# The V blocks of the dense PEER part, issued from ScalarE's DMA queue in place of SyncE's

## The reference, cut to what matters

```python
e = (take_along_axis(si[:, :, 0], ci // 16) * 128 + take_along_axis(si[:, :, 1], ci % 16))
gate = softmax(top)                                     # 128 experts a token
act = gelu(einsum('tkd,td->tk', peer_u[e], ub))         # d = 1024
out = einsum('tk,tkd->td', gate * act, peer_v[e])
```

## Time and profile before

| what | value |
| --- | --- |
| median of 3 runs | 6679.44 us |
| lowest and highest | 6656.4 and 6680.77 us |
| the profiled execution, its own time | 6678.65 us |
| its span, first to last instruction | 6676.6 us |
| mean granted clock of PE | 0.856 of full speed |
| PE, DVE, ACT, POOL busy | 82%, 57%, 18%, 28% |
| gathers (queue q0) | 671.13 MB |
| SP's transfers (queue q1) | 441.96 MB |
| ACT's transfers (queue q10) | 47.99 MB |

### The profile page before, as it was taken

The page is one execution under the profiler, slowest core; times in us unless marked ns, Lnnn a source line. Parts: engine busy times, 40 slices in busy tenths (PEclk is TensorE's granted clock), DMA queues, the critical chain, the costliest instruction groups (busy, mean ns, idle before and its releaser), DMA issues.

```text
span 6676.6 us, 62677 instructions
## 1 busy us (share of the span) xinstructions
PE 5486.7 (82%) x22755; PEld 3635.5 (54%) x22755; DVE 3833.7 (57%) x8953; ACT 1192.3 (18%) x2559; POOL 1875.6 (28%) x1700
## 2 busy tenths in 40 slices
PE   8899877868757779999997899887786668788876
PEld 3699454735554334554552489744655555455554
DVE  1554163737267898876674355342737376766555
ACT  1100032221373000000002110021312450000001
POOL 0000000000487564554551000000001584444442
PEclk9899978778856889999998889899567768898988
DMA  6000101012115999999995200001012249999996
GB/s 210 14 1 1 38 1 32 1 32 63 64 76 238 387 397 389 387 392 358 387 389 206 86 1 1 13 26 32 1 32 64 79 173 374 349 367 369 359 347 245
DMA packets 290066, 1165.07 MB, mean 175 GB/s; under 512 B 24416, under 2 KB 106592, under 8 KB 205024
## 3 DMA queue, kind: packets, MB, share of 16 engines
q0 software_dynamic: 92160, 671.13, 24.9%
q1 hardware_dynamic: 192272, 441.96, 18.9%
q10 hardware_dynamic: 5328, 47.99, 1.7%
HBM read 1116.94 MB, written 44.04 MB: 174 GB/s over the span
## 4 chain that ended last, share of the span: by engine, by line
PE 63%; DMA 13%; DVE 13%; ACT 5%; issue 4%; POOL 1%; ACTq 0%; DVEq 0%; SPq 0%; POOLq 0%
PE psum L413 63%; DMA weight_ring<-in_ut 12%; DVE arena L1261 3%; ACT y_features L975 2%; ACT arena L903 2%; DVE arena L1540 1%; DVE arena L1615 1%; DVE arena L1270 1%; DVE arena L1264 1%; DVE u_features L1267 1%; DVE x_tokens L1261 1%; DVE arena L1382 1%; DVE arena L1267 0%; ACT y_features L977 0%; DVE arena L1357 0%
## 5 line engine op out<-in xcount | busy, mean ns | idle before, releaser
L413 PE MATMUL psum<-u_features,weight_ring 128*128 128x256 f32 (+2 forms) x6464 | 2014.4, 471 | 345.3 <-DMA weight_ring<-in_ut 313.8
L413 PEld LDWEIGHTS psum<-u_features,weight_ring 128*128 128x128 f32 x6464 | 1312.0, 205 | 1074.3 <-DMA weight_ring<-in_ut 361.8
L413 PE MATMUL psum<-weight_ring,consts 128*128 128x512 f32 x2560 | 1141.8, 593 | 2.6 <-DMA weight_ring<-in_uv 1.9
L413 PE MATMUL psum<-arena 128*128 128x64 f32 (+5 forms) x7136 | 983.5, 320 | 45.5 <-DVE arena L1540 23.9
L413 PEld LDWEIGHTS psum<-arena 128*128 128x128 f32 (+2 forms) x7136 | 842.1, 218 | 131.2 <-issue 32.1
L1248 POOL DMA_INDIRECT arena<-in_uv,arena x560 | 833.4, 1488 | 160.4 <-POOL arena L1244 87.2
L413 PEld LDWEIGHTS psum<-weight_ring,consts 128*128 128x128 f32 x2560 | 484.8, 190 | 540.6 <-issue 491.2
L1762 DVE SCALAR_TENSOR_TENSOR y_features<-arena,y_features 128x1024 f32<-128x1024 f32 x560 | 718.0, 1282 | 12.0
L1747 DVE CUSTOM_DVE_ANT_0 arena<-arena,y_features 128x1024 f32<-128x1024 f32 x560 | 665.1, 1219 | 36.7 <-DMA arena<-in_uv,arena 36.6
L1244 POOL TENSOR_TENSOR arena<-consts 128x1 f32<-128x1 f32 x320 | 343.4, 1073 | 1148.5 <-DVE y_features L1762 1125.9
L1230 POOL TENSOR_SCALAR y_features<-consts 128x128 f32<-128x128 f32 x640 | 525.8, 838 | 463.1 <-ACT consts L965 267.7
(11 more groups left out here) (194 smaller groups left out, 5123.1 us busy)
## 6 DMA issues: line engine op xcount, KB each, us to landing
weight_ring<-in_ut SPq DMA_DIRECT2D x256, 512.0 KB, 8.8
weight_ring<-in_uv SPq DMA_DIRECT2D x256, 512.0 KB, 8.6
weight_ring<-in_ws SPq DMA_DIRECT2D x234, 512.0 KB, 3.6
gate_blocks<-arena ACTq DMA_DIRECT2D x20, 2048.0 KB, 6.3
consts<-gate_blocks SPq DMA_DIRECT2D x16, 768.0 KB, 17.3
arena<-gate_blocks SPq DMA_DIRECT2D x16, 768.0 KB, 18.3
arena<-in_uv,arena POOLq DMA_INDIRECT x560, 10.4
consts<-gate_blocks SPq DMA_DIRECT2D x16, 512.0 KB, 15.5
```

Source lines behind the costliest of these rows:

```text
L413: return pe.matmul(o, w, x, start=first, stop=last, skip_group_check=True)
```

## The change

`load_down` moves from SP's program to ACT's. V of block `e` is issued by ACT right behind the gelu of block `e`, for `e` of 2 and more; ACT has at that point already waited for "block added" of `e - 2`, so the buffer is free. V of blocks 0 and 1 is issued by ACT before its first gather group, behind a wait for the weight pieces of the layer. SP keeps a wait for "block added" of `e - 2` where the V load stood, so U loads and gate loads are issued after the same events as before. Sizes, buffers and semaphores are the same.

```diff
@@ SP's program
-                def load_down(e):
-                    if e >= 2:
-                        sp.wait_ge(*at("block added", l, e - 2))
-                    r = l * EXPERTS + e * P
-                    sp.dma_start(DOWN[e % 2], a["uv"][r:r + P, D:2 * D]).then_inc(down_in[e % 2], 16)
...
-                for e in range(2):
-                    load_down(e)
...
                 for e in range(2, BLOCKS):
                     if e + 2 < BLOCKS:
                         load_up(e + 2)
-                    load_down(e)
+                    sp.wait_ge(*at("block added", l, e - 2))
                     if e % QUAD == 2 and 2 <= e // QUAD + 1 < BLOCKS // QUAD:
                         load_gates(e // QUAD + 1)
@@ ACT's program
+            def load_down(l, e):
+                r = l * EXPERTS + e * P
+                act.dma_start(DOWN[e % 2], a["uv"][r:r + P, D:2 * D]).then_inc(down_in[e % 2], 16)
+
             def block_activated(l, e):
...
                 activated(act.activation(HID[e % 2][:, 0:hi - lo], bank(6 + e % 2, 0, hi - lo), ACT.Gelu), "block activated", l, e)
+                if e >= 2:
+                    load_down(l, e)
...
                 gate_weights(l, gather_tiles(l)[0])
+                act.wait_ge(SEM["piece_used"], (l + 1) * PIECES)
+                for e in range(2):
+                    load_down(l, e)
```

## The result

| | before | after |
| --- | --- | --- |
| median | 6680.1 us (4 runs, 6656.4 to 6687.43) | 6853.46 us (4 runs, 6803.99 to 6862.06) |
| ratio, with its 95% interval | | 1.025 (1.0194 to 1.0307) |
| span of the profiled execution | 6676.6 us | 6843.7 us |

The change makes the kernel 2.5% slower. I had forecast 36 us less, 6643 us in a range of 6601 to 6732; it is 173 us more, above the range.

A forecast was written before the change was run, and what follows sets the result against it. PE was taken to wait for U behind slow gate loads, with DMA bytes binding the first stretch. Savings of 30 us in layer 1, 4 and 2 in the second stretch made 36 us off 6678.65: 6643 us, range 6601 to 6732.

The forecast's parts named there:

- What bounds the kernel: Dense parts of both layers: PE waits for U, which stands behind gates slowed by many small packets beside gathers.
- What the change removes: At each gate load, the V 0.37 us ahead no longer delays it; 2.6 us of gather turns can go.
- V moves ahead of the late U: Behind a gate load, V(e + 1) and V(e + 2) may pass U: 2.6 us earlier to 3.0 later, about 1 earlier expected.
- My bound from above: Layer 1's DMA share could rise from 0.92 to 0.97, 60 us; with 18 of the second stretch, 78 us, 6601 us.
- V passes the late U everywhere: Rival, 0.11: two V blocks go ahead of U, 1.7 us later at each of 29 waits, 49 us, 6728 us.
- the second stretch of layer 0: 2556 to 3562 us, PE the bound: 1 us off each of 4 waits, 2 more for sooner U issues.
- ACT is held at the V issue: Rival, 0.11: V issues behind gate loads block ACT, gather gelus and V come late; about 100 us, 6779 us.
- V's cover: PE work before down(e) needs V: 15.5 us in layer 0, 9.8 in layer 1; nothing booked, range widened.
- the bytes moved: Queues: q10 carries about 134 MB more and q1 as much less.
- nothing in the first stretch: 2107 to 2556 us, first gathered tile of layer 0: no gain, as unchanged bytes set the time at DMA share 0.99.
- Nothing to gain: Rival, 0.36: U as late as before, the saving cancelled by V passing U or used up by gathers; 6679 us, within 33.
- the spacer reading: Reading tested in the experiments, not in the prediction: the V ahead of the gate load did some good there.

The follow-up runs named there:

- Long rows: Gate loads read one row of 4 or 6 KB a partition in place of 8 or 12 of 512 bytes, against the kernel before; 6506.41 us, 0.9754.
- 0.8% and 2.6% alone: Against the kernel before: only the V directly ahead of each gate load on ACT, 1.0078; only the other three of each four on ACT, 1.0262.

## Why the prediction was wrong

**What bounds the kernel: right.** U is late because it stands behind the gates, and these are slow because they are many small packets. Long rows, which change nothing but the number of packets (and the pieces of the stores before the dense part), took U waits from 313.8 to 89.7 us and 2.5% off the time. That was the gain in this place, not the queue.

**What the change removes: not there.** I put 2.6 us of gather turns on V ahead of the gates, and booked 1 us of them. With only that V moved, the gates of layer 1 landed 1.5 us earlier (15.8 for 17.3), yet U waits didn't fall (315.9 for 313.8). V and gates share the engines either way.

**The failed step: "V moves ahead of the late U", a range of 2.6 us earlier to 3.0 later, from which I chose 1 us earlier.** Three things in it were wrong. I let V(e + 1) and V(e + 2) cost U "up to 1.5 us" each, as work of their own. But they delay the gates first: while a gate load is under way, its packets share the engines with gathers and now with V as well, and in the cycle shown three V blocks went through: the one that had stood ahead of the gates and the two from behind U. The gates come 6.7 us later in layer 1, and U behind them: 6 us later in the cycle shown, where I had it 1 us earlier. Second, I judged that V(e + 1) starts when the gates are "nearly through", 7 us after them; they took 15 to 17 us, so they were half way. The row was on the table: 15.6 us in the earlier trace rows. Third, I took U waits as the whole price. The gates are needed too: DVE's waits for them went from 169.6 us to 371.8 us in all.

**Missed: what is behind a late transfer is free time that no one can use.** In the old order V stood behind U, so when the gates were through the engines had U, V and gathers to carry and stayed full (1.02 in the 8.9 us behind U's landing). Now U and V have landed, and the gathers have stopped too, since DVE was held by the late gates and POOL by DVE: the engines stand at 0.02 for 3.9 us. That late gates also hold the gathers is in none of my sums. My bound from above asked how far the DMA share could rise (0.92 to 0.97); it fell to 0.87. By 1155 us x 0.92 / 0.87 = 1221 us the same transfers would need 66 us more in layer 1; the stretch is 85 us longer.

**"V passes the late U everywhere": the right mechanism, at 0.11 and mis-sized.** It had the sign and its condition (gates landing over 14 us after their issue) held; the 15.6 us of the earlier trace rows met it before anything ran, so 0.11 was too low by my own working. The price of 1.7 us a wait was for two V blocks less a saving. The excess of U waits is 91 us in layer 1 (I had 49 for 29 waits), and there are 76 us more in the second stretch of layer 0, for which I had booked a gain of 6.

**"ACT is held at the V issue": wrong.** V issues of the dense parts took 0.33 us in the middle and 1.35 at the most, in the row of ACT's V loads after the change (us from the start; durations in ns):

```profile
L986 ACTq DMA_DIRECT2D weight_ring<-in_uv x254: 334/334/1349, 2132.5 to 6796.2; - x127
```

Issues of U on SP are held up to 7.32 us in the same execution; its row for the U loads:

```profile
L363 SPq DMA_DIRECT2D weight_ring<-in_ut x254: 327/328/7322, 2100.8 to 6779.0; - x127
```

And in one place SP was held while ACT was not:

```profile
2178.82 4.18 SPq L363 DMA_DIRECT2D weight_ring<-in_ut  x1
...
2181.42 0.34 ACTq L986 DMA_DIRECT2D weight_ring<-in_uv  x1
```

What held SP there was not shared by the two queues.

**Right, and worth little:** V's cover (PE waits 16.6 us for V in all), the bytes moved, and nothing in the first stretch, where the DMA engines at 0.99 set the time. **"Nothing to gain"**, which the rule of the Trainium skill supported (DMA: Bandwidth & Descriptors, Issuing engines are not separate DMA queues), fell with it, and the measurement decides against the rule: the second queue changed when each transfer got its share, and that cost 2.5% or gave 0.6%, by the packets beside it. The round-robin rule of the same page (Queues, rings and completion order) fits the trace: V blocks on a queue of their own got through whole while a gate load was under way, among them the two that had stood behind it.

**What stays open.** The gate flight grew by 8.6 us in the two cycles compared. V's own 4.1 us on q10, less 0.8 that q1 no longer took, explain 3.3 of them; 4.7 are gather packets, and the rest is idle. No more gathers were asked for: four were issued in either flight. So these packets are those that in the kernel before were still queued when the gates landed; that the gates had to wait for them one by one is argued from the turns and not shown. That the engines idle because V is through and the gathers have stopped is read from one cycle and from the shares; no run forces V to be late with everything else kept, or lets the gathers go on without the gates. And the V ahead of the gates costs 0.8% on ACT (47 us in the medians), of which the rows of its fastest execution show 12 us of span, 2 of U waits and 40 of DVE's waits for gates; where the rest lies I can't say. The kernel with the gate load ahead of V lost the same 0.8%, and it too has no V directly ahead of the gates, so a small part of the spacer reading isn't excluded. The parts don't add up either: 0.8% and 2.6% alone, 2.5% together.

## What to carry to other kernels

A queue that is served in order also keeps a transfer that has time behind one that is late. Before giving it a queue of its own, look at what is slow in the old queue at that moment: the moved transfer takes turns with that, finishes early, and leaves nothing to move when the late one is through. Look too at who waits for the slow load, and which transfers that engine would have started. And where a load of short rows is under way beside transfers with large packets, count its packets times the pair time read from the trace (here 0.31 us): longer rows were worth 2.5%, and decided the sign of the change to the queues.

## What the runs showed of the hardware

The price of a row isn't its bytes. A gate load of 512-byte rows, 0.52 MB in layer 1, took 17.3 us to land, a V block of the same size, issued just ahead of one, 9.5; the same bytes in rows of 1, 2 and 4 to 6 KB took 1.0, 2.0 and 2.5% off the time. A second queue took a real share: three V blocks finished within one gate load that had been issued before them. And the hold on issues was per queue: up to 7.32 us on SP, at most 1.35 on ACT, in one execution, and ACT issued in 0.34 us while SP was held for 4.18.
